# The Hyena mixer transformed by even and odd tokens, with its value chunks right behind their gate chunks

## The chip, the cores and the metric

One NeuronCore of a Trainium2 chip runs the whole program. The metric is the device time in microseconds of one execution, as the median of several runs. TensorE (PE in the profile) does matrix products, VectorE (DVE) and ScalarE (ACT) the work on elements, SyncE (SP) issues most of the transfers.

## The reference, cut to what matters

Two blocks of two layers each work on one sequence of 256 tokens with 1024 features. The last layer's mixer is a Hyena operator:

```python
def hyena_mixer(u, w_in, b_in, conv_w, conv_b, ..., decay, d_bias, w_out, b_out):
    z = dwconv3(u @ w_in + b_in, conv_w, conv_b)      # three taps over tokens
    x1, x2, v = jnp.split(z, 3, axis=-1)
    h_fwd, h_bwd = hyena_filters(L, ..., decay)
    v = v * x2
    y = (two_sided_fftconv(v, h_fwd, h_bwd) + v * d_bias) * x1
    return y @ w_out + b_out
```

The long convolution is a product of spectra: y = inverse(transform(v) * transform(filter)), over twice the sequence's length.

## The kernel before

All weights are in f32. A stream of chunks of 1 MB (128 x 2048) runs through three slots: SyncE loads a chunk into raw (line 595), ScalarE makes its upper part w_hi (hi, line 758), VectorE the lower part w_lo = raw - w_hi (lo, line 1369), and TensorE multiplies with three products per tile (three, line 2264: hi x hi, hi x lo, lo x hi). The chunks have one global number q; hi(q) waits until TensorE has done chunk q-3, and lo(q) for hi(q).

In the Hyena stage the mixer's input projection is 12 chunks of 256 features (hy_in; features lie on partitions, the 256 tokens along the free axis), in the order HY. Chunks 0 to 3 carry x1, chunks 4 to 7 carry x2 (the gates of the values) and 8 to 11 the values v. Each engine runs a loop over j, the place in HY, and its order within an iteration is written out by hand:

- TensorE: feature_chunk(j) into bank 4 or 5, and then what the lists HY_TAPS, HY_FILTER, HY_TURN and HY_SPECTRUM put behind chunk j: the filter taps (line 2786, banks 0 to 3; hid @ w3 for 128 of the 256 tokens), the transform of the filters (spectrum, line 2533, for 512 of the 1024 features each, banks 0 to 3), a turn of one value chunk to tokens on partitions (line 2141), and the transform of the values. Behind the loop come four chunks of inverse products (line 2822, banks 4 and 5) and then the output projection hy_out.
- ScalarE: the chunk plus its bias to z_b (line 1321), hi(q+3), and where the lists say so the window exp (line 1332), copies of the filters' transforms (line 1338), and the copy of a turned chunk (line 1343).
- VectorE: lo(q+3), then the three taps over tokens (lines 2084 and 2088) into z_c, for a value chunk its product with the gate chunk (line 2095), then the filter taps times the window (lines 2102 to 2108), and at the start of the iteration behind a transform of values the complex product (product, lines 2057 to 2064, which reads banks 0 to 3). Behind the loop, for each c: v * d_bias + the inverse, times x1 (lines 2120 and 2125), and hy_lower (line 1725), the lower part that hy_out's products wait for.

The transforms are matrix products with cosines and sines of 256 tokens by 256 bins: `spectrum` has 2 parts (cosine, sine) x 2 halves of bins x 2 halves of tokens = 8 products with 512 columns. An f32 product counts as two records in the profile. The row of a stage by its position:

```python
HY = list(range(4, 12)) + list(range(4))
HY_WINDOW, HY_TAPS, HY_FILTER, HY_TURN, HY_SPECTRUM = [0, 2], [1, 3], [5, 6], [6, 7, 8, 9], [8, 10]
```

A wait in the code is a semaphore: "filter_taps" counts the filter halves that VectorE has finished (the second taps wait for the first), "v_ready" the finished value chunks, "product" the finished complex products, "part_ready" the parts of hy_out's input.

## Time and profile before

| | us |
|---|---|
| median of 3 runs | 1488.92 |
| lowest and highest run | 1486.52, 1498.23 |
| the profiled execution | 1485.65 |
| its span | 1483.7 |
| TensorE busy | 1406.0 |
| VectorE busy | 1130.1 |
| ScalarE busy | 799.3 |

The span is the time from the first to the last instruction of the profiled execution; about 2 us of that execution's time lie around it. Busy times are sums over the span and can overlap between engines. The Hyena stage lies between 1136.8 us (first hy_in product) and 1259.65 us (first hy_out product).

### The profile page before, as it was taken

The numbers are of one execution on the slowest core, as the hardware profiler recorded it, in microseconds if no ns is written. First come the engines' busy times: TensorE is split into PE (matmuls) and PEld (weight loads), VectorE is DVE, ScalarE is ACT, GpSimd is POOL, SyncE is SP. The second block draws the span as 40 slices with busy tenths as digits, with TensorE's granted clock in tenths as the row PEclk, the third lists the DMA queues.
The fourth block names the chain that finished last, engine by engine and source line by source line (L and its number), as shares of the span: only waits on it lengthen the run. The fifth ranks groups of instructions, "written<-read, shape, count | busy, mean of one in ns | idle before, by whom it ended". The sixth has DMA issues, their size and how long they took to land.

```text
span 1483.7 us, 24632 instructions
## 1 busy us (share of the span) xinstructions
PE 1406.0 (95%) x9230; PEld 1184.3 (80%) x9230; DVE 1130.1 (76%) x1705; ACT 799.3 (54%) x1136; POOL 19.6 (1%) x14
## 2 busy tenths in 40 slices
PE   5998899999999899999998899899999999999998
PEld 2874578999966589999797556899997777799997
DVE  6978568888866669988855575798887958676666
ACT  6722465555563665555655674655556432565454
POOL 0002100000000000000001000000000000000000
PEclk9998999999989999999999999999999999999999
DMA  9517729888854658988435002676784433355551
GB/s 377 203 65 270 285 87 385 326 303 311 308 211 164 227 222 343 358 317 343 154 114 171 15 1 90 239 303 256 282 303 147 172 108 114 117 197 179 192 194 57
DMA packets 56761, 315.74 MB, mean 213 GB/s; under 512 B 6867, under 2 KB 9532, under 8 KB 32560
## 3 DMA queue, kind: packets, MB, share of 16 engines
q1 hardware_dynamic: 52530, 303.83, 55.0%
q10 hardware_dynamic: 4158, 10.90, 2.3%
q8 instruction: 50, 0.82, 0.2%
q14 instruction: 23, 0.19, 0.0%
HBM read 311.98 MB, written 1.15 MB: 211 GB/s over the span
## 4 chain that ended last, share of the span: by engine, by line
PE 55%; DVE 6%; ACT 4%; issue 3%; DMA 0%; ACTq 0%; DVEq 0%; SPq 0%
PE bank L2264 47%; PE bank L2533 2%; ACT w_hi L758 1%; DVE w_lo L1369 1%; PE bank L2141 1%; PE bank L2159 1%; DVE small L2010 1%; DVE arena L1398 1%; DVE hf L2027 1%; PE bank L2184 1%; ACT hf L1281 1%; PE bank L2786 0%; PE bank L2822 0%; DMA raw<-in_stream 0%; PE bank L2582 0%
## 5 line engine op out<-in xcount | busy, mean ns | idle before, releaser
L1369 DVE TENSOR_TENSOR w_lo<-raw,w_hi 128x2048 fp32r<-128x2048 f32 x186 | 425.4, 2289 | 160.0 <-ACT w_hi L758 159.2
L2264 PE MATMUL bank<-h_hi,w_hi 128*128 128x256 f32 x1800 | 517.0, 287 | 8.2 <-DVE w_lo L1369 4.1
L2264 PE MATMUL bank<-h_lo,w_hi 128*128 128x256 f32 x1800 | 510.6, 284 | 0.0
L2264 PE MATMUL bank<-h_hi,w_lo 128*128 128x256 f32 x1800 | 510.6, 284 | 0.0
L758 ACT ACTIVATE w_hi<-raw 128x2048 fp32r<-128x2048 f32 x186 | 355.7, 1914 | 105.7 <-PE bank L2264 99.0
L2264 PEld LDWEIGHTS bank<-h_hi,w_hi 128*128 128x128 f32 x1800 | 346.6, 193 | 17.4 <-issue 9.2
L2264 PEld LDWEIGHTS bank<-h_lo,w_hi 128*128 128x128 f32 x1800 | 346.6, 193 | 2.2 <-issue 0.7
L2264 PEld LDWEIGHTS bank<-h_hi,w_lo 128*128 128x128 f32 x1800 | 346.4, 192 | 0.0
L1793 DVE SCALAR_TENSOR_TENSOR arena<-bank,par,arena 128x255 f32<-128x255 f32 (+1 forms) x264 | 109.0, 475 | 84.1 <-ACT arena L1016 67.3
L2264 PE MATMUL bank<-w_hi,a_hi 128*128 128x512 f32 x368 | 146.6, 399 | 6.9 <-DVE a_lo L1818 6.0
L2264 PE MATMUL bank<-w_hi,a_lo 128*128 128x512 f32 x368 | 144.8, 394 | 0.0
L2264 PE MATMUL bank<-w_lo,a_hi 128*128 128x512 f32 x368 | 144.4, 393 | 0.0
L1398 DVE SCALAR_TENSOR_TENSOR arena<-arena,silu_c 128x384 f32<-128x384 f32 (+1 forms) x258 | 140.1, 611 | 1.5 <-ACT arena L1049 1.5
L1016 ACT ACTIVATE arena<-bank,par 128x256 f32<-128x256 f32 x88 | 44.8, 559 | 129.9 <-PE bank L2264 129.9
L2264 PE MATMUL bank<-w_hi,h_hi 128*128 128x512 f32 (+1 forms) x224 | 86.1, 384 | 6.8 <-DVE hf L1582 4.0
L2264 PEld LDWEIGHTS bank<-w_hi,a_hi 128*128 128x128 f32 x368 | 69.9, 190 | 24.2 <-DVE w_lo L1369 7.0
L2264 PE MATMUL bank<-w_hi,h_lo 128*128 128x512 f32 (+1 forms) x224 | 84.2, 376 | 0.0
L2264 PE MATMUL bank<-w_lo,h_hi 128*128 128x512 f32 (+1 forms) x224 | 84.1, 376 | 0.0
L2264 PEld LDWEIGHTS bank<-w_lo,a_hi 128*128 128x128 f32 x368 | 69.8, 190 | 15.2
L2264 PEld LDWEIGHTS bank<-w_hi,a_lo 128*128 128x128 f32 x368 | 70.1, 190 | 13.0
L1034 ACT ACTIVATE a_hi<-arena 128x512 fp32r<-128x512 f32 x44 | 27.8, 632 | 84.2 <-DVE arena L1814 84.1
L2264 PEld LDWEIGHTS bank<-w_hi,h_hi 128*128 128x128 f32 x224 | 42.4, 189 | 18.1 <-issue 10.6
(320 smaller groups left out, 1636.0 us busy)
## 6 DMA issues: line engine op xcount, KB each, us to landing
raw<-in_stream SPq DMA_DIRECT2D x186, 1024.0 KB, 5.1
arena<-in_mod_stream SPq DMA_DIRECT2D x86, 768.0 KB, 7.4
raw<-in_mod_pe SPq DMA_DIRECT2D x36, 512.0 KB, 6.8
arena<-in_mod_later SPq DMA_DIRECT2D x16, 512.0 KB, 6.4
arena<-in_mod_pe SPq DMA_DIRECT2D x12, 512.0 KB, 11.9
sq<-row_store ACTq DMA_DIRECT2D x7, 512.0 KB, 3.7
sq<-in_bias SPq DMA_DIRECT2D x8, 192.0 KB, 6.6
x<-in_x_t ACTq DMA_DIRECT2D x1, 1024.0 KB, 9.8
```

What stands on the lines that cost most here:

```text
L758: nc.scalar.activation(w_hi[s][:], raw[s][:], ACT.Copy).then_inc(hi_done, 1)
L1016: ins = nc.scalar.activation(gate_c[:, e, :], half(4, e), ACT.Identity, scale=par[:, bass.ds(wb[center] + 2 * s + e, 1)], bias=par[:, bass ...
L1034: nc.scalar.activation(slot_hi(q), act_f, ACT.Copy)\
L1281: nc.scalar.activation(mla_s(h, t), bank[u % 4][:], ACT.Exp, bias=small[:, k + 1:k + 2], scale=MLA_SCALE, accum_out=small[:, k + 2:k + 3]) ...
L1369: nc.vector.tensor_tensor(w_lo[s][:], raw[s][:], w_hi[s][:].bitcast(F32), ALU.subtract).then_inc(lo_done, 1)
L1398: ins = nc.vector.scalar_tensor_tensor(parts[e], buf[:, kt % 4, :], silu_c[:, c0 + kt:c0 + kt + 1], parts[e], ALU.mult, ALU.add)
L1793: ins = nc.vector.scalar_tensor_tensor(o, src, par[:, bass.ds(w[tap] + 2 * s + e, 1)], o, ALU.mult, ALU.add)
L2010: link(nc.vector.tensor_reduce(small[:, k:k + 1], bank[u % 4][:], AX_X, ALU.max))
L2027: nc.vector.tensor_scalar(mla_s(h, t), mla_s(h, t), small[:, k + 3:k + 4], None, ALU.mult)\
L2141: return nc.tensor.transpose(out_, in_, ident[0:n, 0:n])
L2264: ins = nc.tensor.matmul(out_, l, r, start=first and n == 0, stop=last and n == 2, **kw)
L2533: ins = nc.tensor.matmul(bank[2 * part + ft][:], dft[:, part, t, ft * P:(ft + 1) * P], sources[part][:, t, 512 * s_:512 * s_ + 512], start ...
```

## The change

With half-odd bins the second 128 bins of a transform of 256 tokens follow from the first 128: the even tokens' sums are the same up to a sign, and so are the odd tokens'. The changed kernel transforms even and odd tokens apart, for 128 bins each (spectrum: 4 products of 128 x 512 for 8), and builds both sets of bins with sums and differences on VectorE (both_bins), for the filters in filter_bins and for the values at the start of product. ScalarE copies the values' transforms from the banks to SBUF first (hy_bins). The product ends with four more sums and differences, so that the inverse too (token_mix) is done by parity: 8 products with 128 columns for a chunk, for 8 with 256. The inverses go to banks 0 to 3, the first two of them behind chunk 9; mixed reads them by pairs of tokens. The value chunks stand right behind their gate chunks in HY. Taps, filters, turns and the values' transforms move to earlier places in the lists. The centre tap of the convolution moves from VectorE to ScalarE, which reads each half of the chunk's bank twice; two operations on 24 columns fold the input bias into the convolution's. lo(q+3) moves from the head of VectorE's iteration to behind the convolution and the gate product. mixed 0 and 1 stand behind VectorE's iterations 9 and 10, hy_lower 0 and 1 ahead of mixed 2 and 3. ScalarE's loads of the gate rows wait for the second product.

```diff
@@ -96,10 +96,9 @@
             turn[b + 24 + i, b + 16 + i] = -1
             turn[b + 16 + i, b + 24 + i] = 1
-    w = 2 * np.pi * np.outer(t, np.arange(T) + 0.5) / (2 * T)
...
           ("ffn3", 3 * FT // 2))
-HY = list(range(4, 12)) + list(range(4))
...
             return sq[:, 4 * (h % 2):4 * (h % 2) + 4, :]
+
+        def by_pairs(k):
+            return z_c[:, k, :].rearrange("p (m b) -> p m b", b=2)
+
+        hy_bins = [[hf[:, 4 * i + 2 * b:4 * i + 2 * b + 2, :].rearrange(flat) for b in range(2)] for i in range(2)]
         def kv_part(v):
...
         PART = {"glu": [1, 2], "attention": [3, 6], "ssm": [4, 5], "mla_out": [7, 8, 9, 10], "hy_out": [11, 12, 13, 14]}
-        HY_WINDOW, HY_TAPS, HY_FILTER, HY_TURN, HY_SPECTRUM = [0, 2], [1, 3], [5, 6], [6, 7, 8, 9], [8, 10]
+        HY_WINDOW, HY_TAPS, HY_FILTER, HY_TURN, HY_SPECTRUM = [0, 1], [1, 2], [3, 4], [3, 4, 6, 8], [5, 8]
...
                 for e in range(2):
-                    c0 = COL["hy_b_in_2"] + 2 * c + e
+                    k = 2 * c + e
+                    c0, w1, cb = COL["hy_b_in_2"] + k, COL["hy_conv_w_2"] + 24 + k, COL["hy_conv_b_2"] + k
+                    nc.scalar.activation(z_c[:, k, :], half(4 + fill % 2, e), ACT.Identity, scale=par[:, w1:w1 + 1], bias=par[:, cb:cb + 1])
                     ins = nc.scalar.activation(z_b[j % 2][:, e, :], half(4 + fill % 2, e), ACT.Identity, bias=par[:, c0:c0 + 1])
                 ins.then_inc(bank_free, 1)
...
+                    act.wait_ge(sem("transformed"), n + 1)
+                    for i, f in enumerate((f_re, f_im)):
+                        for b in range(2):
+                            ins = nc.scalar.activation(f[:, b, 512 * n:512 * n + 512], bank[2 * i + b][:], ACT.Copy)
+                    ins.then_inc(sem("parts_copied"), 1)
...
-            act.wait_ge(sem("hy_taps"), 2)
+                if j in HY_SPECTRUM:
+                    n = HY_SPECTRUM.index(j)
+                    act.wait_ge(sem("transformed"), n + 3)
+                    if n:
+                        act.wait_ge(sem("product"), n)
+                    for i, v in enumerate(hy_bins):
+                        for b in range(2):
+                            ins = nc.scalar.activation(v[b], bank[2 * i + b][:], ACT.Copy)
+                    ins.then_inc(sem("parts_copied"), 1)
+            act.wait_ge(sem("product"), 2)
...
+            cw, cb = COL["hy_conv_w_2"], COL["hy_conv_b_2"]
+            center_w, center_b = par[:, cw + 24:cw + 48], par[:, cb:cb + 24]
+            in_b = par[:, COL["hy_b_in_2"]:COL["hy_b_in_2"] + 24]
+            link(nc.vector.tensor_tensor(hy_center[:], in_b, center_w, ALU.mult))
+            nc.vector.tensor_tensor(center_b, center_b, hy_center[:], ALU.add)
             norm_x(12)
             mod_out(1, [(4, 16, 48)])
-            cw, cb = COL["hy_conv_w_2"], COL["hy_conv_b_2"]
+            def both_bins(re, im):
+
+                nc.vector.tensor_tensor(re[0], re[0], re[1], ALU.add)
+                link(nc.vector.tensor_tensor(im[0], im[0], im[1], ALU.add))
+                nc.vector.scalar_tensor_tensor(re[1], re[1], -2.0, re[0], ALU.mult, ALU.add)
+                return nc.vector.scalar_tensor_tensor(im[1], im[1], 2.0, im[0], ALU.mult, ALU.subtract)
+
+            def filter_bins(n):
+
+                dve.wait_ge(sem("parts_copied"), n + 1)
+                part = slice(512 * n, 512 * n + 512)
+                both_bins(*([f[:, b, part] for b in range(2)] for f in (f_re, f_im))).then_inc(sem("filter_ready"), 1)
+
             def product(n):
-                dve.wait_ge(sem("spectrum"), n + 1)
                 dve.wait_ge(sem("filter_ready"), 2)
                 part = slice(512 * n, 512 * n + 512)
-                for ft in range(2):
-                    fr, fi = f_re[:, ft, part], f_im[:, ft, part]
-                    ur, ui = bank[ft][:], bank[2 + ft][:]
-                    p0, p1, p2, p3 = (tiles_of(hf, i).rearrange("p a b -> p (a b)") for i in range(4))
-                    nc.vector.tensor_tensor(p0, ur, fr, ALU.mult)
-                    real = chain.on(nc.vector.tensor_tensor(p1, ui, fi, ALU.mult))
-                    nc.vector.tensor_tensor(p2, ur, fi, ALU.mult)
-                    imag = chain.on(nc.vector.tensor_tensor(p3, ui, fr, ALU.mult))
-                    chain_wait(real)
-                    link(nc.vector.tensor_tensor(y_re[:, ft, part], p0, p1, ALU.subtract))
+                dve.wait_ge(sem("parts_copied"), n + 3)
+                v_re, v_im = hy_bins
+                p0, p1, p2, p3 = (tiles_of(sq, i).rearrange("p a b -> p (a b)") for i in range(4))
+                link(both_bins(v_re, v_im))
+                for b in range(2):
+                    fr, fi = f_re[:, b, part], f_im[:, b, part]
+                    nc.vector.tensor_tensor(p0, v_re[b], fr, ALU.mult)
+                    nc.vector.tensor_tensor(p1, v_im[b], fi, ALU.mult)
+                    nc.vector.tensor_tensor(p2, v_re[b], fi, ALU.mult)
+                    imag = chain.on(nc.vector.tensor_tensor(p3, v_im[b], fr, ALU.mult))
                     chain_wait(imag)
-                    ins = nc.vector.tensor_tensor(y_im[:, ft, part], p2, p3, ALU.add)
-                    if ft == 0:
-                        link(ins)
-                ins.then_inc(sem("product"), 1)
+                    nc.vector.tensor_tensor(v_re[b], p0, p1, ALU.subtract)
+                    link(nc.vector.tensor_tensor(v_im[b], p2, p3, ALU.add))
+                nc.vector.tensor_tensor(y_re[:, 0, part], v_re[0], v_re[1], ALU.add)
+                nc.vector.tensor_tensor(y_re[:, 1, part], v_re[0], v_re[1], ALU.subtract)
+                nc.vector.tensor_tensor(y_im[:, 0, part], v_im[0], v_im[1], ALU.subtract)
+                nc.vector.tensor_tensor(y_im[:, 1, part], v_im[0], v_im[1], ALU.add).then_inc(sem("product"), 1)
                 dve.wait_ge(sem("product"), n + 1)
+
+            def mixed(c):
+
+                dve.wait_ge(sem("hy_conv"), 9 + c)
+                dve.wait_ge(sem("hy_y_done"), c + 1)
+                for e in range(2):
+                    k = 2 * c + e
+                    c0 = COL["hy_d_bias_2"] + k
+                    ins = nc.vector.scalar_tensor_tensor(by_pairs(DT + k), by_pairs(2 * DT + k), par[:, c0:c0 + 1],
+                                                         half(c, e).rearrange("p (b m) -> p m b", b=2), ALU.mult, ALU.add)
+                link(ins)
+                k = 2 * c
+                nc.vector.tensor_tensor(z_c[:, DT + k:DT + k + 2, :], z_c[:, DT + k:DT + k + 2, :], z_c[:, k:k + 2, :], ALU.mult)\
+                    .then_inc(sem("hy_y_ready"), 1)
...
                 q, fill = Q["hy_in"] + j, FILL["hy_in"] + j
+                if j - 1 in HY_FILTER:
+                    filter_bins(HY_FILTER.index(j - 1))
                 if j - 1 in HY_SPECTRUM:
                     product(HY_SPECTRUM.index(j - 1))
-                lo_upto(q + 3)
...
                 n = [0, 0]
-                for tap, d in ((1, 0), (0, 1), (2, -1)):
+                for tap, d in ((0, 1), (2, -1)):
                     for e in range(2):
...
                         w = par[:, cw + 24 * tap + k:cw + 24 * tap + k + 1]
-                        if tap == 1:
-                            ins = nc.vector.tensor_scalar(z_c[:, k, :], zb[:, e, :], w, par[:, cb + k:cb + k + 1], ALU.mult, ALU.add)
...
+                        if tap:
                             chain_wait(n[e])
-                            o, i_ = (z_c[:, k, 1:], zb[:, e, 0:T - 1]) if d > 0 else (z_c[:, k, 0:T - 1], zb[:, e, 1:])
-                            ins = nc.vector.scalar_tensor_tensor(o, i_, w, o, ALU.mult, ALU.add)
-                        if tap != 2:
+                        o, i_ = (z_c[:, k, 1:], zb[:, e, 0:T - 1]) if d > 0 else (z_c[:, k, 0:T - 1], zb[:, e, 1:])
+                        ins = nc.vector.scalar_tensor_tensor(o, i_, w, o, ALU.mult, ALU.add)
+                        if not tap:
                             n[e] = chain.on(ins)
...
+                lo_upto(q + 3)
...
                     nc.vector.tensor_tensor(hy_d[:, t, :], hy_fwd, hy_bwd, ALU.subtract).then_inc(sem("filter_taps"), 1)
+                if j in (9, 10):
+                    mixed(j - 9)
...
-                if c:
-                    hy_lower(c - 1)
+            hy_lower(0)
+            hy_lower(1)
+            mixed(2)
+            mixed(3)
+            hy_lower(2)
             hy_lower(3)
...
                 for part in range(2):
-                    for ft in range(2):
-                        for t in range(2):
-                            ins = nc.tensor.matmul(bank[2 * part + ft][:], dft[:, part, t, ft * P:(ft + 1) * P],
-                                                   sources[part][:, t, 512 * s_:512 * s_ + 512], start=(t == 0), stop=(t == 1))
+                    for parity in range(2):
+                        i = 2 * part + parity
+                        ins = nc.tensor.matmul(bank[i][:], dft[:, i, :], sources[part][:, parity, 512 * s_:512 * s_ + 512], start=True, stop=True)
...
+            def token_mix(c):
+                pe.wait_ge(sem("parts_copied"), 4)
+                pe.wait_ge(sem("product"), c // 2 + 1)
+                for e in range(2):
+                    k = 2 * c + e
+                    for parity in range(2):
+                        out_ = half(c, e)[:, parity * P:(parity + 1) * P]
+                        for part, y in enumerate((y_re, y_im)):
+                            ins = nc.tensor.matmul(out_, y[:, parity, k * P:(k + 1) * P], idft[:, 2 * part + parity, :],
+                                                   start=(part == 0), stop=(part == 1))
+                ins.then_inc(sem("hy_y_done"), 1)
+
...
-                        ins = nc.tensor.matmul(bank[b][:], hid[1][:, t * P:(t + 1) * P], w3[:, 512 * b:512 * b + 512], start=True, stop=True)
+                        ins = nc.tensor.matmul(bank[b][:], hid[1][:, t::2], w3[:, 512 * b:512 * b + 512], start=True, stop=True)
...
-                        pe.wait_ge(sem("filter_ready"), 1)
-                    spectrum((hy_s, hy_d), n).then_inc(sem("filter_done"), 1)
+                        pe.wait_ge(sem("parts_copied"), 1)
+                    spectrum((hy_s, hy_d), n).then_inc(sem("transformed"), 1)
...
-                            ins = turn(bank[6 + n % 2][:, t * T + e * P:t * T + (e + 1) * P], z_c[:, 2 * DT + 2 * n + e, t * P:(t + 1) * P])
+                            ins = turn(bank[6 + n % 2][:, t * T + e * P:t * T + (e + 1) * P], by_pairs(2 * DT + 2 * n + e)[:, :, t])
...
-                    pe.wait_ge(sem("filter_ready"), 2)
+                    pe.wait_ge(sem("parts_copied"), n + 2)
                     pe.wait_ge(sem("hy_v_ready"), 2 * n + 2)
-                    if n:
-                        pe.wait_ge(sem("product"), 1)
-                    spectrum((hy_v, hy_v), n).then_inc(sem("spectrum"), 1)
...
-                ins.then_inc(sem("hy_y_done"), 1)
+                    spectrum((hy_v, hy_v), n).then_inc(sem("transformed"), 1)
+                if j == 9:
+                    token_mix(0)
+                    token_mix(1)
+            token_mix(2)
+            token_mix(3)
             projection("hy_out", part_of("hy_out"))
```

## Rows read from the trace of the kernel before

**Rows 1.** The page: busy time by engine; the chain that ended last.

```profile
PE 1406.0 (95%) x9230; PEld 1184.3 (80%) x9230; DVE 1130.1 (76%) x1705; ACT 799.3 (54%) x1136; POOL 19.6 (1%) x14
...
PE 55%; DVE 6%; ACT 4%; issue 3%; DMA 0%; ACTq 0%; DVEq 0%; SPq 0%
```

**Rows 2.** Windows of the Hyena stage: length, busy (count) by engine, clock, DMA.

```profile
1136.80:1259.65 122.85, 120.37 (x739) 98.01 (x739) 94.57 (x150) 49.47 (x65) 0.00 (x0) 1.00 0.39 137
1250.00:1259.65 9.65, 7.17 (x33) 6.03 (x33) 7.22 (x16) 1.89 (x3) 0.00 (x0) 1.00 0.23 95
```

**Rows 3.** Waits in 1136 to 1260 us: total, times, longest.

```profile
ACT arena L1321 <- PE bank L2264: 52.9, 11, 10.0
DVE w_lo L1369 <- ACT w_hi L758: 24.4, 8, 7.8
...
PE bank L2822 <- DVE arena L2120: 1.3, 1, 1.3
PE bank L2264 <- DVE arena L2120: 1.2, 1, 1.2
```

**Rows 4.** TensorE's groups in 1136.8 to 1259.65 us.

```profile
L2533 PE MATMUL bank<-arena 128*128 128x512 f32 x64 | 28.1, 592 | 0.0
L2822 PE MATMUL bank<-arena 128*128 128x256 f32 x64 | 14.2, 380 | 1.3 <-DVE arena L2120 1.3
L2786 PE MATMUL bank<-sq,arena 64*128 64x512 f32 x16 | 7.4, 602 | 0.0
L2141 PE MATMUL bank<-ident_sb,arena 128*128 128x128 f32 x16 | 2.4, 273 | 0.0
```

**Rows 5.** VectorE's groups in the same stretch.

```profile
L2088 DVE SCALAR_TENSOR_TENSOR arena<-arena,par 128x255 f32<-128x255 f32 x48 | 20.0, 479 | 0.0
L2084 DVE TENSOR_SCALAR arena<-arena,par 128x256 f32<-128x256 f32 x24 | 8.8, 408 | 0.0
```

**Rows 6.** VectorE's timeline: start, length, line, what, count, idle before.

```profile
1157.75 0.68 DVE L2102 TENSOR_TENSOR arena<-bank,hf 128x512 f32<-128x512 f32 x1
...
1162.58 1.22 DVE L2108 TENSOR_TENSOR arena<-arena 128x1024 f32<-128x1024 f32 x1
...
1218.59 0.69 DVE L2057 TENSOR_TENSOR hf<-bank,arena 128x512 f32<-128x512 f32 x1
...
1225.55 0.69 DVE L2064 TENSOR_TENSOR arena<-hf 128x512 f32<-128x512 f32 x1
...
1250.32 0.87 DVE L2120 SCALAR_TENSOR_TENSOR arena<-arena,par,bank 128x256 f32<-128x256 f32 x2
1251.23 0.69 DVE L2125 TENSOR_TENSOR arena<-arena 128x512 f32<-128x512 f32 x1
1251.84 0.86 DVE L2120 SCALAR_TENSOR_TENSOR arena<-arena,par,bank 128x256 f32<-128x256 f32 x2
```

**Rows 7.** ScalarE's timeline, the same columns.

```profile
1179.41 0.84 ACT L1321 ACTIVATE arena<-bank,par 128x256 f32<-128x256 f32 x2 [3.12 <-PE bank L2264]
...
1186.28 2.07 ACT L1338 ACTIVATE arena<-bank 128x512 f32<-128x512 f32 x4 [4.23 <-PE bank L2533]
1192.04 0.84 ACT L1321 ACTIVATE arena<-bank,par 128x256 f32<-128x256 f32 x2 [3.69 <-PE bank L2264]
```

**Rows 8.** Windows around TensorE's idle stretches, same columns (PE, PEld, DVE, ACT, POOL, clock).

```profile
176.00:179.00 3.00, 0.75 (x4) 0.47 (x5) 1.11 (x2) 2.94 (x8) 0.00 (x0) 1.00 1.00 421
420.00:429.00 9.00, 8.39 (x25) 5.75 (x26) 6.37 (x18) 7.10 (x18) 0.00 (x0) 0.50 0.12 34
801.00:804.50 3.50, 0.00 (x0) 0.00 (x0) 3.38 (x6) 1.23 (x4) 0.00 (x0) 1.00 0.62 215
805.00:808.00 3.00, 2.90 (x7) 2.36 (x8) 1.12 (x1) 1.85 (x2) 0.00 (x0) 0.50 0.55 199
1120.00:1122.00 2.00, 0.00 (x0) 0.00 (x0) 2.00 (x1) 2.00 (x2) 0.00 (x0) 1.00 0.97 381
1123.00:1124.00 1.00, 1.00 (x3) 0.81 (x4) 1.00 (x1) 0.86 (x2) 0.00 (x0) 0.50 0.36 143
```

More of the change, by code:

```diff
@@ L97, in consts @@
             turn[b + 16 + i, b + 24 + i] = 1
[L99 to L102 removed]
+    w = 2 * np.pi * np.outer(t, np.arange(P) + 0.5) / (2 * T)
+    waves = [f(w[parity::2]) for f in (np.cos, np.sin) for parity in range(2)]
+    fwd, back = np.concatenate(waves, 1), np.concatenate([v.T / T for v in waves], 1)
     theta = 2 * np.pi * (np.arange(BINS) + 0.5) / (2 * BINS)
@@ L138 @@
           ("ffn3", 3 * FT // 2))
-HY = list(range(4, 12)) + list(range(4))
+HY = [4, 8, 5, 9, 6, 10, 7, 11] + list(range(4))
 def tiled(w):
@@ L1334, in _ @@
                     n = HY_FILTER.index(j)
-                    act.wait_ge(sem("filter_done"), n + 1)
-                    for part, dst in enumerate((f_re, f_im)):
-                        for ft in range(2):
-                            ins = nc.scalar.activation(dst[:, ft, 512 * n:512 * n + 512], bank[2 * part + ft][:], ACT.Copy)
-                    ins.then_inc(sem("filter_ready"), 1)
+                    act.wait_ge(sem("transformed"), n + 1)
[3 more added lines that the diff above has]
+                    ins.then_inc(sem("parts_copied"), 1)
                 if j in HY_TURN:
```

41 lines of the change are left out of this document (7 added, 34 removed).

## The prediction

> **What bounds the kernel now.** I read the page's first and fourth parts first [rows 1]: TensorE is busy 95% of the span and the chain that ended last is mostly TensorE, so the kernel gains only where TensorE's own order gets shorter. The change touches one stage, the Hyena mixer of the last layer, from the first hy_in chunk (1136.8 us) to the first hy_out product (1259.65). The windows of that stretch [rows 2] show TensorE busy 120.37 of 122.85 us, all at full granted clock; VectorE is busy 94.57 and ScalarE 49.47. TensorE's only holes are in the last 9.65 us. The waits [rows 3] say the same: VectorE and ScalarE wait for TensorE (ScalarE 52.9 us for chunks, VectorE 24.4 for upper parts), TensorE waits 1.3 and 1.2 us for VectorE, both at the inverse products. So the stage is TensorE-bound with VectorE 28 us behind it: a change that takes 20 us from TensorE and gives VectorE more work moves the bound, and the order of VectorE's queue has to be followed.
>
> **What TensorE loses.** The transforms: 64 records of 128x512 in 28.1 us [rows 4] are four calls of spectrum (two filters, two signals), 7.0 us each; ScalarE's rows give 6.87 (1186.28 minus 1179.41, [rows 7]). Even and odd tokens each need one product in place of two, so 3.43 stays: 4 x 3.44 = 13.7 us less. The inverse: 64 records of 128x256 in 14.2 us are 3.5 us for each of 4 chunks. After, as many instructions (8 a chunk, 16 records) with 128 columns: half is 1.75, and the transposes of 128x128 [rows 4], 2.4 us for 16, bound one record from above by 0.15, so 2.4 a chunk. I take 1.95, 6 us less in all. Chunks (5.76, 1192.04 minus 1186.28 in [rows 7]; I reckon 5.8), filter taps (7.4 us for two, 3.63 each used) and turns keep their work. Together 19.7 us: if nothing else ended late, 1466.
>
> **What VectorE gets.** Off: the centre tap on VectorE, 24 x 0.37 = 8.8 us [rows 5], now a second activation per half on ScalarE. On: filter_bins, 4 operations of 512 elements twice. A 512-element operation advances the queue by 0.6 us, and by 0.71 with a link behind it: twelve of them with four links are 7.65 us (1218.59 to the end at 1226.24, [rows 6]). So filter_bins is 2.65 each. The product goes from 12 to 20 operations: 2.75 (bins), 2 x 3.8, 2.4 = 12.8 us, 5.1 more, twice. Sum for VectorE: -8.8 + 5.3 + 10.3 = +6.8 us, 101 of a stretch of 117 to 123. That is nearly full, so where it sits decides. The products now read copies in SBUF, where an operation costs what it does from a bank (0.69 both, [rows 6]). The scalar_tensor_tensor of 512 elements has no row; from 255 elements at 0.48 with the queue moving every 0.4 (20.0 us busy for 48, [rows 5]) it lies between 0.6 and 0.8 of queue time. I take 0.67; there are eight, so -0.5 to +1 us.
>
> **What ScalarE gets.** Four activations per chunk for two (0.84 the pair, [rows 7]), some 0.8 more a chunk, and eight copies of spectra for the products, 1.93 to 2.07 a set [rows 7]. It is busy 49 of 123 us [rows 2]; it is late only where a chain runs through it. The two small operations for the folded bias stand ahead of norm_x(12): under 0.4 us, behind the row turns of TensorE; taken as 0, at most 0.4.
>
> **The queues, in order.** I wrote down each engine's instructions in its own order with these durations and the waits of the code. For the kernel before this gives the start of hy_out at 1258.8 where the trace has 1259.65; I use differences only. For the changed one:
> First, taps 1 move from behind chunk 3 to behind chunk 2. Their products need banks 0 to 3, which VectorE leaves when it has used taps 0. VectorE starts those at 1157.75 now and ends near 1163.8 [rows 6]; after the change conv 1, the v product and lo 4 stand ahead of them, which comes to 1157.7, the same. TensorE has finished chunk 2 at 1158.2 and is idle 5.4 us, until 1163.8. Before, chunk 3 filled exactly this hole. What is late next is everything TensorE does.
> Second, from taps 1: taps, chunk 3, filter 0 (0.3 us for the rows that turn 0 waits for), turn, chunk 4, filter 1, turn, chunk 5 are 29.1 us at full clock, none waits for VectorE (its filter_bins end 3 us before chunk 5's data). Then spectrum 0, 3.43. VectorE does conv 5, v, lo 8 and enters product 0 some 6.3 us after chunk 5; it ends 19.1 after it. Behind it wait conv 6, lo 9, conv 7 and the last v product: 25.2 after chunk 5. TensorE has done chunks 6, 7, 8 at 21.4: it is idle 3.9 us before turn 3. lo 9 and lo 10, moved behind the convolutions, land in time.
> Third, turn 3, ScalarE's copy, spectrum 1 and its copies (0.44 + 0.7 + 3.43 + 1.95) put product 1 6.5 us later. Then VectorE has no hole: product 12.8, then conv 9, 10, 11 (1.6 each), lo 12, 13, 14 (2.2 each), mixed 0 and 1 (1.5 each, [rows 6]) and the first lower, 15.1 us. TensorE has finished inverses 2 and 3 five microseconds before that: third idle stretch, 4.9 us, against 2.5 of idle there before. hy_lower(0) and (1) stand ahead of mixed 2 and 3, which hide under the first hy_out chunk.
> Sum without anything else: -13.7 - 6.0 + 5.4 + 0.3 + 4.6 (3.9 and the copy's 0.7) + 2.4 is -7.0; the queues written out in full, with the longer activations, give -5.6.
>
> **The clock.** TensorE's granted clock follows its idle stretches in this trace [rows 8]. After 3.5 us of idle from 801 the clock is 0.5 (the lower of its levels, 1.2 of 2.4 GHz) for 3 us of nearly full work; behind the 2 idle microseconds from 1120 it is 0.5 at 1123. With thin work behind the idle it stayed at 0.5 for 9 us (420 to 429). The holes now in the Hyena stage (1.3 and 1.2 us) cost none: 1.00 throughout [rows 2]. The change makes three holes of 5.4, 3.9 and 4.9 us. I take 3.5 us at half speed behind each, a loss of 1.75 us of work, three times 1.75 = 5.2: the first passes on whole, the second sits under turn and spectrum 1 (on the path), the third under the first hy_out products. -5.6 + 5.2 = -0.4 us.
>
> One page speaks against the change and changes no sum here. mixed reads its bank with the two parities interleaved, 128 columns apart; no row here reads a bank so, and I bound its two bank reads (0.9 of its 1.5 us, [rows 6]) between that and double, 0 to +1.8 us on the path through mixed 0 and 1, and take 0, since bank reads in order cost what SBUF reads do. The Trainium skill (SBUF — State Buffer, Door 1: The DMA port swizzle) says that PSUM has lines of 8 bytes and that any non-contiguous access to it slows matmuls, and that SBUF allows four fp32 per 16-byte line for free, so the pair-wise weight loads would cost nothing. By the first these reads would lie at the upper end; nothing in the trace of before can show it.
>
> **The rivals.**
> A (forecast, 0.5): idle and slow clock eat the saving. 1485.65 - 0.4 = 1485.3 against the profiled execution; its own range is -3 to +2.
> B, 0.27: the holes are there but the clock stays up behind some of them, or VectorE is a little faster than in my sum (12.0 a product): -5.6 to -7.2, so 1478.5 to 1480. For it: 2.25 us of idle in the 3 us from 176 kept the clock at 1.00 [rows 8]. Against: the holes there nearer in length to these lost it.
> C, 0.18, slower: half clock lasts, as at 420 to 429, because what follows the holes is transposes and short products with waits between them (turn 3, copy, spectrum 1). Every microsecond more of half speed at each of three places costs 1.5; the sign turns at 3.8 us each, and at 7 us each it is +4.9, 1490.5. The interleaved bank read adds up to 1.8.
> D, 0.05: the saving arrives nearly whole (VectorE keeps ahead because filter taps 1 or the last v product are not waited for): -15 to -19.7, 1466 to 1470. Against it: the wait for filter_taps stands in the code and VectorE's 5.96 us of taps work are in [rows 6]. That the change does not do what it says (transforms as long as before, weight loads with stride 2 as the limit) belongs here too with the other sign: +4 to +10; I leave it inside C.
>
> **How the numbers follow.** The median of the runs before, 1488.92, is 3.3 us above the profiled execution (1485.65). On the scale of the median: A 1488.5, B 1482 to 1483, C 1490 to 1496, D 1470 to 1473. The predicted time is A's. The range, 1481 to 1495, takes A and B whole and most of C, and is 1.5 for the runs' own scatter wider on the low side; D and the far part of C stay out. About 1% (15 us) is what a measurement of this kernel can tell from no change; only D reaches that on one side and almost nothing on the other: faster 0.05, same 0.92, slower 0.03.
>
> **What the profile after would show.** TensorE idle 5 to 6 us ahead of the second filter taps, released by VectorE; 3 to 5 ahead of the fourth turn; 4 to 5 ahead of hy_out, released by the first hy_lower; clock 0.5 behind each. Transforms 32 records in 14 us; inverses 7 to 9.5 us in all. VectorE's products 12 to 14 us each, without holes from product 1 to the end of the lowers. The forecast is wrong if the first hole is missing, if the clock reads 1.00 after them (then B), or if the interleaved additions take over 0.6 us each (then C).

## The result and the profile after

The changed kernel takes 1499.85 us, median of 13 runs (1495.92 to 1504.56); the kernel before, on the same chip in turn with it, 1494.86 us (13 runs). The ratio, worked out from all runs and not as the quotient of the two medians (which is 1.0033), is 1.0038 [1.0023, 1.0053]: 5.7 us slower (0.0038 of 1494.86), where -0.4 was forecast. The rest of the distance to 1488.5 is the yardstick: the three runs shown ahead had the median 1488.92, thirteen have 1494.86, 5.9 us more.

The page of the changed kernel, busy time by engine and the chain that ended last; it answers to [rows 1]:

```profile
PE 1395.5 (93%) x9184; PEld 1178.4 (79%) x9198; DVE 1137.8 (76%) x1707; ACT 814.0 (54%) x1168; POOL 19.6 (1%) x14
...
PE 49%; DVE 10%; ACT 5%; issue 4%; DMA 0%; ACTq 0%; DVEq 0%; SPq 0%
```

TensorE is busy 10.5 us less and VectorE 7.7 more, and VectorE's share of the chain rose from 6% to 10%, TensorE's fell from 55% to 49%. TensorE has room now, and something else sets its times. The span is 1497.6 for 1483.7, but 9.0 of those 13.9 us lie ahead of the stage: its first product starts at 1145.82 for 1136.80. This part of the program is the same in both but for two small operations on 24 columns, and in two traces of the kernel before alone its length differs by 7.35 us (experiment 12), so spans of two traces can't be compared here; stages can. The windows of the changed kernel (columns as in [rows 2]): the Hyena stage to the first hy_out product, the stretches around TensorE's three idle ones, and the first half of hy_out:

```profile
1145.82:1271.01 125.19, 108.01 (x708) 91.06 (x707) 99.12 (x144) 63.67 (x96) 0.00 (x0) 0.91 0.36 125
...
1168.00:1170.00 2.00, 0.00 (x0) 0.00 (x0) 1.73 (x4) 2.00 (x4) 0.00 (x0) 1.00 1.02 291
1171.00:1183.00 12.00, 9.93 (x21) 5.34 (x22) 8.33 (x12) 0.00 (x0) 0.00 (x0) 0.50 0.27 91
1232.00:1239.00 7.00, 4.83 (x9) 2.43 (x10) 6.96 (x9) 1.27 (x2) 0.00 (x0) 0.52 0.77 260
1270.00:1276.00 6.00, 4.99 (x12) 3.96 (x13) 5.84 (x12) 1.26 (x2) 0.00 (x0) 0.50 0.59 205
...
1271.01:1284.63 13.62, 13.62 (x48) 10.70 (x48) 11.48 (x15) 3.18 (x3) 0.00 (x0) 0.81 0.24 81
```

Up to the first hy_out product the stage took 122.85 us and takes 125.19, though TensorE is busy 12 us less in it. The mean clock says why: 0.91 for 1.00. It stands at 0.50, the lower of its two levels (1.2 GHz), from 1171 to past 1183, for most of 1232 to 1239 and from 1270 to 1276. The last of these stretches lies mostly behind hy_out's start, in the first half of hy_out, which takes 13.62 us for the 11.15 of before. So I measure from the first hy_in product to the last product of hy_out: 151.00 us for 146.15, or +4.85. What follows is 200.8 us in both traces: what the change does lies in the stage.

The waits of the changed kernel in the stage, columns as in [rows 3]:

```profile
PE bank L2302 <- DVE h_lo L1741: 5.9, 1, 5.9
PE bank L2835 <- DVE arena L2155: 5.7, 1, 5.7
...
PE bank L2179 <- DVE arena L2141: 4.3, 1, 4.3
...
PE bank L2571 <- ACT arena L1350: 0.8, 1, 0.8
```

These are the three holes, by the releasers named ahead: second filter taps 5.7 (line 2155 of VectorE makes the taps), fourth turn 4.3 and 0.8 for the copy behind it, hy_out 5.9 (line 1741 makes the lower part). Forecast: 5.4, 3.9 and 0.7, 4.9.

TensorE's groups in the stage, answering to [rows 4]:

```profile
L2571 PE MATMUL bank<-arena 128*128 128x512 f32 x32 | 16.2, 653 | 0.8 <-ACT arena L1350 0.8
L2835 PE MATMUL bank<-sq,arena 64*128 64x512 f32 x16 | 10.9, 838 | 5.7 <-DVE arena L2155 5.7
L2819 PE MATMUL bank<-arena 128*128 128x128 f32 x64 | 7.5, 275 | 0.0
L2179 PE MATMUL bank<-ident_sb,arena 128*128 128x128 f32 x16 | 3.1, 325 | 4.7 <-DVE arena L2141 4.3 <-ACT mod_rows L820 0.4
```

The transforms went from 64 records to 32, the inverses from 14.2 us to 7.5 (1.9 a chunk). The filter taps are the same 16 records as before, yet 10.9 us for 7.4, and the turns 3.1 for 2.4: that is the clock, visible in a group whose work did not change. TensorE's timeline shows it product by product (start, length; the last column is the idle time before):

```profile
1173.07 7.16 PE L2835 MATMUL bank<-sq,arena 64*128 64x512 f32 x8 [5.74 <-DVE arena L2155]
...
1183.96 0.37 PE L2302 MATMUL bank<-h_hi,w_lo 128*128 128x256 f32 x1
1184.17 0.28 PE L2302 MATMUL bank<-h_hi,w_hi 128*128 128x256 f32 x1
1184.28 0.28 PE L2302 MATMUL bank<-h_lo,w_hi 128*128 128x256 f32 x1
```

Behind the hole the taps take 7.16 us (3.63 at full clock), then chunk 3's products follow each other every 0.21 us until 1184, and every 0.12 from there (0.11 in the last pair). The chunk takes 7.6 us for 5.8. Between 1173.07 and 1184 TensorE had no gap: 11 us of uninterrupted work at half speed.

VectorE's timeline, answering to [rows 6]:

```profile
1214.25 0.69 DVE L2070 TENSOR_TENSOR hf<-hf 128x512 f32<-128x512 f32 x1
...
1215.57 0.69 DVE L2072 SCALAR_TENSOR_TENSOR hf<-hf 128x512 f32<-128x512 f32 x1
1216.18 0.68 DVE L2073 SCALAR_TENSOR_TENSOR hf<-hf 128x512 f32<-128x512 f32 x1
...
1226.43 0.69 DVE L2101 TENSOR_TENSOR arena<-hf 128x512 f32<-128x512 f32 x1
...
1259.60 0.87 DVE L2111 SCALAR_TENSOR_TENSOR arena<-arena,par,bank 128x256 f32<-128x256 f32 x2
```

VectorE's terms were sized well: scalar_tensor_tensor of 512 elements is 0.69 us like its neighbours and moves the queue by 0.61 (1215.57 to 1216.18) for the 0.67 taken, a product 12.87 us (1214.25 to 1227.12) for the forecast 12.8, and the interleaved bank reads of line 2111 take 0.87 the pair, what the ordered ones took [rows 6].

### The profile page after: what moved, and what is told of

Same layout as the page of the kernel before. It is cut to its first block, busy times and chain, and to the rows that moved or that the text cites. A ratio compares the mean times of both kernels' runs of the same rounds, so it can differ in the third digit from the quotient of the medians.

```text
span 1497.6 us, 24589 instructions
## 1 busy us (share of the span) xinstructions
PE 1395.5 (93%) x9184; PEld 1178.4 (79%) x9198; DVE 1137.8 (76%) x1707; ACT 814.0 (54%) x1168; POOL 19.6 (1%) x14
## 4 chain that ended last, share of the span: by engine, by line
PE 49%; DVE 10%; ACT 5%; issue 4%; DMA 0%; ACTq 0%; DVEq 0%; SPq 0%
PE bank L2302 44%; DVE w_lo L1385 2%; ACT w_hi L763 1%; ACT hf L1286 1%; DVE arena L2134 1%; DVE hf L2043 1%; DVE small L2026 1%; PE bank L2179 1%; DVE arena L1414 1%; PE bank L2619 1%; DVE hf L1598 1%; PE bank L2571 1%; PE bank L2197 1%; DMA raw<-in_stream 0%; PE bank L2835 0%
```

## The experiments

"Stage" below is always first hy_in product to last hy_out product in the profiled execution. A "hole" is a stretch in which TensorE is idle. The first time given is the median; ratios need not be the quotient of two medians (0.9993 in experiment 1, where the ratio is 0.9973). They compare with the kernel before on the same chip (medians 1494.06, 1494.18 and 1494.02 in the three sets).

**1. All three holes kept busy.** TensorE multiplies a tile of zeros (bf16, 512 columns) into a bank that is free, in each hole.

```diff
                     if t:
+                        stay_awake(24, 7)
                         pe.wait_ge(sem("filter_taps"), 1)
 ...
+                    if n == 3:
+                        stay_awake(17, 7)
                     pe.wait_ge(sem("v_ready"), n + 1)
 ...
+            stay_awake(24, 7)
             projection("hy_out", ...)
```

> The changed kernel with products of zeros (128x512 bf16, into bank 7) in TensorE's three holes of the Hyena stage: 24 ahead of the wait for filter_taps, 17 ahead of the fourth turn, 24 ahead of the output projection. Nothing else moves. Clock theory: the changed kernel loses by the half clock behind the holes (11 us at 0.5 behind the first, some 5 behind each of the others: 9 to 10 us of work in all), the holes themselves it can afford. Then the granted clock is 1.00 from the first hy_in product to the end of hy_out and the kernel is 7 to 10 us faster than the changed one, at a ratio of 0.996 to 0.999 to the kernel before. Rival, VectorE's queue: the stage's length is set by VectorE's order, so a faster TensorE behind the holes only waits longer: less than 3 us gained, ratio 1.002 to 1.004.

Measured: 1493.01 us, ratio 0.9973 [0.995, 0.9996]. Windows (its stage to hy_out) and waits of this kernel:

```profile
1147.92:1265.73 117.81, 114.76 (x773) 93.67 (x772) 99.12 (x144) 63.71 (x96) 0.00 (x0) 1.00 0.38 134
```

```profile
PE bank L2302 <- DVE hf L1598: 1.6, 1, 1.6
...
PE bank L2302 <- DVE h_lo L1741: 0.7, 1, 0.7
PE bank L2179 <- DVE arena L2141: 0.6, 1, 0.6
PE bank L2836 <- DVE arena L2155: 0.5, 1, 0.5
```

The zeros compute nothing that is used, and VectorE's busy time is the same 99.12, yet the stage is 141.75 us instead of 151.00. 9.25 us is thus what the half clock cost, and 117.81 to hy_out is 5.04 below before's 122.85: the sum without the clock (-5.6) held up to there. Of the 5.04, 4.4 are left at the stage's end (141.75 for 146.15); the wait of 1.6 ahead of the second half of hy_out (for the reads of line 1598), 1.04 in before, took the other 0.6.

**2. Only the first hole kept busy.** The first insertion of experiment 1 alone.

> The changed kernel with the 24 products of zeros ahead of the wait for filter_taps alone. Clock theory: the first hole's half clock passes on whole, since TensorE waits for nobody in the 30 us behind it: 4 to 5.5 us less than the changed kernel, ratio 1.000 to 1.001. VectorE's queue theory: under 2 us, ratio above 1.002.

Measured: 1495.07 us, ratio 1.0005 [0.9985, 1.0026]; stage 145.49, 5.5 less than changed. A window behind the second hole, and the waits:

```profile
1225.00:1234.00 9.00, 7.51 (x15) 3.60 (x16) 6.64 (x7) 0.72 (x2) 0.00 (x0) 0.62 0.76 264
```

```profile
PE bank L2302 <- DVE h_lo L1741: 5.9, 1, 5.9
PE bank L2179 <- DVE arena L2141: 4.3, 1, 4.3
```

The other two holes are unchanged to 0.1 us and the clock falls behind both. The first hole alone cost 5.5 of the 9.25 us, which is half of the 11 us that its slow clock lasted; the other two together 3.7, near the forecast 3.5.

**3. The new arithmetic in the order of before.** It tells the products saved from the order changed.

```diff
-HY = [4, 8, 5, 9, 6, 10, 7, 11] + list(range(4))
+HY = list(range(4, 12)) + list(range(4))
-... HY_TURN, HY_SPECTRUM = [0, 1], [1, 2], [3, 4], [3, 4, 6, 8], [5, 8]
+... HY_TURN, HY_SPECTRUM = [0, 2], [1, 3], [5, 6], [6, 7, 8, 9], [8, 10]
 (inverses, mixed and lower parts behind the last chunk, as before)
```

> The changed kernel's arithmetic (even and odd tokens, bins on VectorE, centre tap on ScalarE, lower parts behind the convolution) in the order of the kernel before: value chunks behind all gate chunks, windows, taps, filters, turns and spectra in the old places, all four inverses behind the loop. Order theory: the moves opened the holes, the arithmetic saves. Taps 1 are not waited for, no hole until the second product, then one hole of some 10 us while VectorE does the 12.9 us of product 1. Laid out by durations: 5.6 us less than the kernel before, less 2 to 5 for the half clock behind that hole, which lies mostly on VectorE's path: ratio 0.996 to 0.999. Rival, arithmetic theory: the added 17 us of work on VectorE cost what TensorE saves in any order: ratio 1.002 or more.

Measured: 1489.05 us, ratio 0.996 [0.9942, 0.9978]; stage 138.79. Its one hole, by the waits:

```profile
PE bank L2816 <- DVE arena L2101: 11.0, 1, 11.0
```

This divides the change in two. The arithmetic, with the centre tap on ScalarE and the lower parts behind the convolution, takes 7.4 us off the stage (146.15 to 138.79); the new lists and places put 12.2 back (to 151.00). With the old order all of VectorE's lateness stands in one place, ahead of the third inverse, with one stretch of slow clock behind it, in which TensorE works for 6.1 us (1256.27 to 1262.37). What that stretch costs this kernel wasn't measured.

**4. The new order with the second taps behind chunk 3.** Chunk 3 fills the first hole again; the turns and spectra keep early places.

```diff
-... = [0, 1], [1, 2], [3, 4], [3, 4, 6, 8], [5, 8]
+... = [0, 1], [1, 3], [5, 6], [3, 4, 7, 8], [7, 10]
-                if j == 9:
+                if j == 10:
                     token_mix(0)
 ...
-                if j in (9, 10):
-                    mixed(j - 9)
+                if j in (10, 11):
+                    mixed(j - 10)
```

> The changed kernel with the value chunks behind their gates, but the second taps behind chunk 3 as before, filters behind 5 and 6, turns behind 3, 4, 7, 8, spectra behind 7 and 10, the first two inverses behind chunk 10 and their mixed in VectorE's iterations 10 and 11. Order theory: no hole ahead of taps or turns, one of 2 us ahead of the first inverses and one of some 8 ahead of the third: 6 to 7 us less than the kernel before laid out by durations, ratio 0.995 to 0.998. Arithmetic theory: ratio 1.002 or more. If it is no better than the old order with the same arithmetic, the early value chunks buy nothing.

Measured: 1486.94 us, ratio 0.9947 [0.9927, 0.9968]; stage 137.95. Waits:

```profile
PE bank L2819 <- DVE arena L2101: 7.1, 1, 7.1
PE bank L2819 <- ACT hf L1359: 2.2, 1, 2.2
```

The first hole is gone and nothing took its place; what is left up to hy_out, 9.3 us, stands ahead of inverses, where VectorE's products (line 2101 is a product's last operation) and the copies for them end. It beats both kernels.

**5. Experiment 4 with its holes kept busy.**

```diff
                 if j == 10:
+                    stay_awake(8, 7)
                     token_mix(0)
                     token_mix(1)
+            stay_awake(31, 7)
             token_mix(2)
```

> The kernel with the second taps behind chunk 3 (run e4_taps_behind_three) and products of zeros in its two remaining holes: 8 ahead of the first inverses, 31 ahead of the third (7.1 us idle there in its trace, clock 0.5 until 1259). Clock theory: the half clock in that run cost about 1.5 us of inverses behind the first hole and 2 to 3 behind the second, on the path: another 2 to 4 us less, ratio to the kernel before 0.992 to 0.994. VectorE theory: behind product 1 VectorE's chain (chunk 11's convolution, lower part, mixed, lower) sets hy_out's start whatever the clock: 0 to 1.5 us less, ratio 0.994 to 0.995.

Measured: 1485.6 us, ratio 0.995 [0.9927, 0.9973]; to hy_out 113.35 us at clock 1.00 (114.06 at 0.94 in experiment 4), whole stage 138.30 (137.95). A window of this kernel, the stretch behind hy_out's start:

```profile
1255.00:1259.00 4.00, 3.87 (x10) 3.12 (x11) 3.85 (x8) 0.85 (x3) 0.00 (x0) 0.57 0.52 217
```

Two slow stretches ahead of hy_out had cost 0.7 us in all, since they stood where VectorE was late anyway: TensorE at full speed only reaches the next wait sooner, here one of 2.2 us for the first lower part, and behind that one the clock fell. The clock is a loss where TensorE is the bound behind the hole, not everywhere.

**6. The centre tap alone moved to ScalarE**, in the kernel before.

```diff
+                    nc.scalar.activation(z_c[:, k, :], half(4 + fill % 2, e), ACT.Identity, scale=par[:, w1:w1 + 1], bias=par[:, cb:cb + 1])
                     ins = nc.scalar.activation(z_b[j % 2][:, e, :], ...)
 ...
-                for tap, d in ((1, 0), (0, 1), (2, -1)):
+                for tap, d in ((0, 1), (2, -1)):
```

> The kernel before with one part of the change alone: the centre tap computed by ScalarE from the bank (24 more activations, 24 tensor_scalar fewer on VectorE), the input bias folded by two small operations. The stage before is TensorE-bound, VectorE waits 24 us in it: no gain, and at most 1 us lost by ScalarE's later release of the banks: ratio 0.998 to 1.002. Rival: TensorE's end of stage (inverse products wait for VectorE behind product 1) gains the 0.7 us a chunk of VectorE work behind product 1: up to 1.5 us, ratio 0.998 to 0.999.

Measured: 1497.56 us (median of 11 runs; one more took 2763.88 us and stands outside the median and the ratio), ratio 1.0019 [0.9998, 1.0039]; stage 147.53, +1.4. Windows and waits:

```profile
1139.03:1263.25 124.22, 120.42 (x740) 98.02 (x740) 86.90 (x126) 60.38 (x89) 0.00 (x0) 1.00 0.39 135
```

```profile
PE bank L2827 <- DVE arena L2125: 1.6, 1, 1.6
...
PE bank L2791 <- DVE arena L2113: 1.1, 1, 1.1
```

VectorE is 7.7 us freer and the end is no sooner: TensorE was the bound, as [rows 2] said. A new wait of 1.1 stands before the second taps; one activation more per half of a chunk lengthens the way from a chunk to its convolution. By itself this part is a small loss by the stage; the ratio's interval includes 1. That it pays where VectorE sets the end follows from the price found in experiment 7 and wasn't run.

**7. Experiment 5 without the bins in product** (part of the transform's work is left out, so this is a probe of price and no version).

```diff
-                link(both_bins(v_re, v_im))
```

> As e5_best_awake, but without the first four operations of each complex product (the sums and differences that make both sets of bins of the values), so the result is not the reference's; it prices VectorE's added work. VectorE theory: the stage ends with VectorE's chain, so 2.75 us less in each of two products comes out nearly whole: 4 to 5.5 us less than e5, ratio about 0.003 lower. Clock or TensorE theory: under 1.5 us.

Measured: 1481.84 us, ratio 0.9908 [0.9881, 0.9934]. The window of its stage to hy_out:

```profile
1151.12:1260.63 109.51, 108.70 (x746) 91.29 (x747) 93.74 (x136) 63.58 (x96) 0.00 (x0) 1.00 0.43 146
```

VectorE loses 5.1 us of work and hy_out starts 3.84 sooner (3.05 at the stage's end), somewhat less than the 4 to 5.5 expected. Shown with this: in the better order VectorE's chain sets the stage; a microsecond less there is worth 0.75 at hy_out's start and 0.6 at the stage's end.

**8. Experiment 4 with the lower part of the weights made ahead of the convolution.**

```diff
+                lo_upto(q + 3)
                 dve.wait_ge(bank_free, fill + 1)
 ...
-                lo_upto(q + 3)
                 if j in HY_TAPS:
```

> As e4_taps_behind_three, but with the lower part of chunk j+3 back at the head of VectorE's iteration, as in the kernel before, ahead of the convolution. It tells what this one move of the change is worth. Order laid out by durations: the filter taps' products start 2.2 us later than TensorE needs them behind chunk 3 and the last value product too, 2 to 4 us slower than e4, ratio 0.996 to 0.998. Rival: it changes nothing, because VectorE does the same work in either order: ratio 0.994 to 0.995.

Measured: 1493.77 us, ratio 0.9991 [0.9969, 1.0012]; stage 145.85, 7.9 us over experiment 4. Waits:

```profile
PE bank L2819 <- DVE arena L2101: 5.9, 1, 5.9
PE bank L2819 <- ACT hf L1359: 5.5, 1, 5.5
PE bank L2835 <- DVE arena L2155: 1.8, 1, 1.8
```

It costs twice what was expected, and the clock falls behind each of the three holes. The three are 13.2 us for the 9.3 of experiment 4: the second taps are waited for again (1.8), and the copies for the values' second transform, which stand behind the first product, are 5.5 us late ahead of the first inverses instead of 2.2. That is about half of the 7.9. TensorE works some 18 us at half clock in these stretches for 9 in experiment 4, which by estimate is the other half. In this order, then, the lower part behind the convolution is a good part of the change.

**9. Experiment 5 with the shortest chain to hy_out.** mixed(1) and the first two lower parts stand directly behind the second product, and the lower part of the third hy_out chunk's weights behind all of hy_out's own.

```diff
                     product(HY_SPECTRUM.index(j - 1))
+                if j == 11:
+                    mixed(1)
+                    hy_lower(0)
+                    hy_lower(1)
 ...
+                if j < 11:
                     lo_upto(q + 3)
```

> As e5_best_awake (second taps behind chunk 3, holes filled), with VectorE's order behind the second product shortened: mixed 1 and the first two lowers directly behind product 1, then chunk 11's convolution, mixed 2 and 3, lowers 2 and 3, and the lower part of the third hy_out chunk behind them. The work is the same. VectorE theory: hy_out's start is product 1's end plus what VectorE still has ahead of the first lower; that falls from 6.3 us to 2.1, and the last two inverses (3.8 us) become the last thing: hy_out starts 3.8 to 4.0 us behind product 1 in place of 6, stage 2 to 2.6 us shorter than e5, ratio to the kernel before 0.992 to 0.994. TensorE or clock theory: under 0.7 us.

Measured: 1485.9 us, ratio 0.9944 [0.9924, 0.9965]. hy_out starts after 110.91 us, 2.44 sooner than in experiment 5, as expected; the stage ends at 139.13, 0.8 later. VectorE's timeline under hy_out says where it went:

```profile
1258.69 2.29 DVE L1385 TENSOR_TENSOR w_lo<-raw,w_hi 128x2048 fp32r<-128x2048 f32 x1
1260.89 1.22 DVE L1906 TENSOR_TENSOR sq<-sq 128x1024 f32<-128x1024 f32 x1
1262.15 2.36 DVE L1908 TENSOR_TENSOR x<-x,sq 128x1024 f32<-128x1024 f32 x2
1264.54 2.29 DVE L1385 TENSOR_TENSOR w_lo<-raw,w_hi 128x2048 fp32r<-128x2048 f32 x1
1266.75 0.68 DVE L1598 TENSOR_TENSOR hf<-bank,sq 128x512 f32<-128x512 f32 x1
```

No row has idle time before it: VectorE has no hole up to the reads of line 1598, which free the bank for the second half of hy_out. TensorE waits 4.3 us for them, and behind that wait its clock falls once more:

```profile
1271.00:1272.00 1.00, 1.00 (x4) 0.81 (x3) 0.69 (x1) 0.99 (x2) 0.00 (x0) 0.50 0.11 41
```

Moving VectorE's work out of the way of hy_out's start puts it in the way of hy_out's middle.

**10. The same without zeros.** The edit of experiment 9 in experiment 4.

> The same order without any products of zeros. The hole ahead of the third inverse is followed by half clock; now the inverses stand directly on the path, so the half clock costs their doubling (3.7 us at most 7) and part of hy_out: 2 to 4 us slower than e9 in the stage, so about as fast as e4_taps_behind_three, ratio 0.993 to 0.996. If the clock did not matter here it would equal e9.

Measured: 1485.66 us, ratio 0.9951 [0.993, 0.9971]; stage 137.74 (experiment 4: 137.95). Waits:

```profile
PE bank L2823 <- DVE arena L2101: 8.3, 1, 8.3
PE bank L2306 <- DVE hf L1598: 2.3, 1, 2.3
```

The expectation missed: 2 to 4 us slower than experiment 9 by stage, and it is 1.4 shorter. hy_out does start 2.2 us later (113.10 for 110.91). But the wait for line 1598 is then 2.3 us and the clock stays up behind it, where in experiment 9 it was 4.3, with 3.4 us of half clock behind it. The zeros thus bought an earlier start of hy_out and lost it again behind it.

Experiments 4, 5, 9 and 10 end within 1.4 us of each other by stage and by median: four ways to lay the same amount of VectorE work.

**11 and 12. The changed kernel and the kernel before again**, each with one empty line more, for the profile alone.

> The changed kernel unaltered, for one more trace: are the half clock's lengths behind the holes (11, 5 and 5 us in the first trace) and the stage's 151.0 us from first hy_in to last hy_out product the same in another execution? Clock theory: the three holes are there to a tenth of a microsecond, the lengths at 0.5 vary by some us, the stage is between 147 and 152 us.

> The kernel before unaltered, for one more trace: the stage (146.15 us in the first) and the part behind it (200.75 us) should repeat to 0.3 us, since the clock is 1.00 in them; the part ahead of the stage, with idle stretches and half clock, should vary by several us and hold the scatter of the runs.

Measured: stages 151.13 and 146.15 us (151.00 and 146.15 in the first traces). A window of the changed kernel's second trace, the slow stretch behind its first hole:

```profile
1171.00:1183.00 12.00, 11.79 (x32) 7.20 (x33) 8.33 (x12) 0.00 (x0) 0.00 (x0) 0.52 0.25 87
```

Windows of the second trace of before, the stage and the work behind the idle stretch ahead of it (that of 1120 in [rows 8]):

```profile
1144.15:1267.00 122.85, 120.37 (x739) 98.01 (x740) 94.60 (x150) 49.49 (x65) 0.00 (x0) 1.00 0.39 136
...
1129.00:1134.00 5.00, 5.00 (x12) 3.94 (x13) 3.31 (x3) 1.56 (x4) 0.00 (x0) 0.50 0.11 43
```

The 11 us are no accident of one trace. The stage of before repeats exactly; its start came 7.35 us later than in the first trace, all of the 7.4 between the spans (1491.1 and 1483.7). In that part of the program TensorE has many idle stretches, and the slow clock behind the same one lasts over 5 us here where it lasted about 3 there.

| kernel | stage, us | ratio |
|---|---|---|
| before | 146.15 | 1 |
| changed | 151.00 | 1.0038 |
| 1 three holes filled | 141.75 | 0.9973 |
| 2 first hole filled | 145.49 | 1.0005 |
| 3 old order | 138.79 | 0.996 |
| 4 taps behind chunk 3 | 137.95 | 0.9947 |
| 5 the same, holes filled | 138.30 | 0.995 |
| 6 centre tap alone | 147.53 | 1.0019 |
| 7 a probe, bins left out | 135.25 | 0.9908 |
| 8 lower part first | 145.85 | 0.9991 |
| 9, 10 short chain | 139.13, 137.74 | 0.9944, 0.9951 |

## Why the prediction was wrong

**What failed is one term, the clock: "I take 3.5 us at half speed behind each, a loss of 1.75 us of work, three times 1.75 = 5.2".** The mechanism (holes, then a slow clock) was right, and the size came from the nearest row only (801 to 808 in [rows 8]). Behind the first hole half clock lasted 11 us of full work and cost 5.5 (experiment 2) for 1.75, passed on whole as forecast; the other two cost 3.7 together for 3.5. 9.25 in place of 5.2 (experiment 1) makes -0.4 into +3.7. The other 1.2 of the measured +4.85 is the sum without the clock: -4.4 at the stage's end (141.75 for 146.15) for -5.6. The three holes are 1.8 us longer together than forecast (16.7 for 14.9).

**Rival C was what happened**, with 0.18: half clock lasts longer and the kernel is slower. Its +4.9 is the measured +4.85 by its number and not by its way: it had 7 us at each of three places and blamed the thin work behind the holes, and it was 11 behind the first, with full work there, and 5 to 6 behind the others. The row that said so was in [rows 8]: 9 us at 0.50 from 420, with TensorE busy 8.39 of 9.00 us. I called the work behind that idle thin and set the row aside; it is 93% busy, and the missing 0.6 us is the end of the idle stretch itself. Microsecond by microsecond, in the trace of before:

```profile
418.00:419.00 1.00, 1.00 (x3) 0.15 (x1) 0.96 (x3) 0.76 (x3) 0.00 (x0) 1.00 0.00 0
419.00:420.00 1.00, 0.29 (x1) 0.00 (x0) 0.93 (x4) 0.72 (x2) 0.00 (x0) 0.65 0.00 0
...
421.00:422.00 1.00, 1.00 (x7) 1.00 (x6) 0.93 (x4) 1.00 (x3) 0.00 (x0) 0.50 0.02 4
```

The idle stretch was 1.3 us (419.30 to 420.61), the clock fell at its start, and TensorE worked from its end on without a gap until past 429. The other two idle stretches were read short as well, since their windows lie inside them: 4.4 us ahead of 805.10 for the "3.5", and 3.2 ahead of 1122.84 for the "2". The mean of the 9 us from 420 and the 3.5 taken from 805 is 6.25 us, 3.1 lost at each of three holes, and -5.6 + 9.4 = +3.8: the right sign, from rows that were there. None of the three signs that the prediction named for being wrong came true (the first hole is there, the clock falls, an interleaved addition takes 0.44 us): they asked whether the clock falls and not for how long.

**TensorE's loss** was right: the transforms 16.2 us for 28.1 with part of them at half speed, the inverses 1.9 a chunk for the forecast 1.95. **VectorE's gain** was right: its stage work is 99.12 us up to hy_out, and two mixed of 1.5 each now lie behind it, 102 for the forecast 101; over the whole program it is busy 7.7 us more for the forecast 6.8. **The queues in order** were right: all three holes stand where they were put, with the releasers named, 0.3 to 1.0 us longer; without the clock they give -5.04 for the forecast -5.6 (experiment 1). **The interleaved read** cost nothing, as was taken, and not the up to 1.8 us of the upper bound; **scalar_tensor_tensor** moves the queue by 0.61 for the 0.67 taken. **B** (clock stays up) is refuted; experiment 1 is the kernel it describes, and it is 4.4 us shorter than before by stage. **D** fell with the holes.

**The time itself** missed by 11.35 us (1499.85 for 1488.5). 5.94 of that is the median of before, which three runs put lower than thirteen did; 4.99, the difference of the two medians, and the forecast 0.42 are the change.

**A question that the prediction didn't ask** was whether the order itself was worth its place. It costed the change as a whole against before; experiment 3 shows a saving of 7.4 us with the old order and a loss of 12.2 from the new one. Of the 12.2 between 6.2 and 9.25 is clock, by estimate: the 9.25 of the changed kernel, less what half clock costs experiment 3, at most half of its 6.1 us.

## What to carry to other kernels

Where TensorE is the bound and a move opens holes in its stream, price each hole twice: its length, and half of the slow stretch behind it. Take that stretch from the nearest row for one end of the range and from the longest row for the other; here this gives -0.4 to +7.9 us (-5.6 and three times 4.5), and +4.85 was measured. Holes can be left where the work behind them waits for another engine anyway (experiment 5), so gather them there (experiments 3 and 4), or fill them with idle products (experiment 1). When TensorE's work shrinks until another engine is the bound, that engine's total and order set the end (experiments 7 and 8), and a shorter chain to one point can come back at the next (experiment 9).

## What the runs showed of the hardware

How long the granted clock stays at 0.50 isn't fixed: about 3 us behind the hole at 1120 in one trace of before and over 5 behind the same in another, 11 us behind the first hole of the changed kernel in both of its traces, though TensorE worked without a gap. What sets the length stays open. Nor is it fixed which holes it follows. In the stages traced here holes of up to 1.6 us were never followed by 0.50 and unfilled ones of 4.3 us and more always. Between them it went both ways: 1.8 us was followed by 7 us of it in experiment 8 (ahead of the second taps), by 3.4 in experiment 7 and by none at a second place in experiment 8; 2.2 us was followed by 3.4 in experiments 4 and 5; 2.2 and 2.3 us in experiment 10 by none. Ahead of the stage even a shorter hole came with it: the one of 1.3 us near 420 came with 10 us at 0.50, counted from its start, in three of the four traces of before and the changed kernel, and with none in the fourth. Windows of experiment 8 and of experiment 10, behind such a hole each:

```profile
1181.00:1188.00 7.00, 7.00 (x26) 5.03 (x25) 6.96 (x13) 0.66 (x2) 0.00 (x0) 0.56 0.70 238
```

```profile
1228.00:1232.00 4.00, 4.00 (x36) 4.00 (x37) 4.00 (x6) 0.00 (x0) 0.00 (x0) 1.00 0.75 268
```

Where two traces of one kernel differ, they differ ahead of the stage: those of before by 7.35 us there and by nothing in the stage, where the clock is at 1.00, and those of the changed kernel by 1.9 us there. Ahead of the stage the clock was at 0.50 for 48 us in one trace of before and for 58 in the other; by estimate that is up to 5 of the 7.35 us, and the rest stays open. Both pairs of stages agree to 0.13 us or better, while the interval of the 13 runs is 4.5 us wide (1.0023 to 1.0053).
